# Early reads of the routed results, a regrouped front, and one gate-up moved ahead of the shared expert in a two-layer trunk kernel

## The reference

```python
def trunk_layer(x, cvec, l, lp, ctx, row, col):
    mod = jax.nn.silu(cvec) @ lp['w_mod'] + lp['b_mod']
    sh1, sc1, g1, sh2, sc2, g2 = jnp.split(mod[:, None, :], 6, axis=-1)
    h = rms_norm(x, lp['g_pre1']) * (1.0 + sc1) + sh1
    m, new_cache = token_mixers(h, lp, lam_init, ctx, row, col)
    x = x + g1 * rms_norm(m, lp['g_post1'])
    h = rms_norm(x, lp['g_pre2']) * (1.0 + sc2) + sh2
    x = x + g2 * rms_norm(moe(h, lp), lp['g_post2'])

def moe(h, lp):          # 32 experts, 4 chosen for each token, and one shared expert
    ...
    gu = jnp.einsum('nd,edf->nef', t, lp['w_exp_gu'])
    a = jax.nn.silu(gu[..., :EXPERT_FF]) * gu[..., EXPERT_FF:]
    a = (a * combine[..., None].astype(a.dtype)).reshape(-1, N_EXPERTS * EXPERT_FF)
    routed = a @ lp['w_exp_down'].reshape(N_EXPERTS * EXPERT_FF, D_MODEL)
    sgu = t @ lp['w_sh_gu']
    shared = (jax.nn.silu(sgu[:, :SHARED_FF]) * sgu[:, SHARED_FF:]) @ lp['w_sh_down']
    return (routed + shared).reshape(B, T, D)
```

## Time and profile before

| | |
|---|---|
| three runs | 2102.24, 2106.28, 2112.89 us (median 2106.28) |
| profiled execution | 2108.57 us, its span 2106.4 us |
| PE, PE weight loads, DVE, ACT, POOL busy | 89%, 66%, 61%, 49%, 21% of the span |
| mean granted TensorE clock | 0.948 |
| weights of the experts | 128 gate-up and 64 down transfers of 1 MB |
| reads of `y_rows` | 12 transfers of 1 MB |

### The profile page before, as it was taken

One profiled execution on the slowest core, in us unless ns is written; L12 is line 12 of the kernel. 1 busy time (PEld: TensorE's weight loads), 2 busy tenths in 40 slices (PEclk: granted clock), 3 DMA queues, 4 the chain that ended last, 5 costly groups with the idle time before them and its releaser, 6 DMA issues. The chain is left out here.

```text
span 2106.4 us, 27239 instructions
## 1 busy us (share of the span) xinstructions
PE 1884.7 (89%) x9282; PEld 1393.5 (66%) x9282; DVE 1283.1 (61%) x1827; ACT 1040.4 (49%) x1713; POOL 451.5 (21%) x422
## 2 busy tenths in 40 slices
PE   4999899899998999999649999979999799999991
PEld 2987566788877566666438865668888666666661
DVE  2244567644436688888753455675444467888885
ACT  2333235633335478777533412464333437787782
POOL 0001511310000434444200043114000042343430
PEclk8999999999998999999869999999999989999996
DMA  7534464133334599999834434503333248999984
GB/s 259 175 120 123 154 226 156 47 120 120 121 109 181 178 359 354 345 348 347 295 99 143 136 118 143 200 6 98 123 120 120 106 174 309 355 351 339 350 313 177
DMA packets 145349, 416.91 MB, mean 198 GB/s; under 512 B 26704, under 2 KB 37232, under 8 KB 119152
## 3 DMA queue, kind: packets, MB, share of 16 engines
q1 hardware_dynamic: 125136, 379.76, 51.8%
q0 software_dynamic: 17952, 33.74, 4.8%
q10 hardware_dynamic: 2176, 2.27, 0.4%
HBM read 408.80 MB, written 32.15 MB: 209 GB/s over the span
## 5 line engine op out<-in xcount | busy, mean ns | idle before, releaser
L1648 DVE TENSOR_TENSOR W_split<-W,W_split 128x2048 fp32r<-128x2048 f32 (+2 forms) x92 | 216.2, 2352 | 423.8 <-ACT W_split L1253 423.8
L2190 PE MATMUL psum<-W_split,qT_split 128*128 128x512 f32 (+3 forms) x1536 | 411.4, 380 | 16.2 <-PEq L2519 8.0
L1253 ACT ACTIVATE W_split<-W 128x2048 fp32r<-128x2048 f32 (+2 forms) x92 | 170.0, 1854 | 385.2 <-PE psum L2190 385.2
L2190 PEld LDWEIGHTS psum<-W_split,qT_split 128*128 128x128 f32 x1536 | 284.7, 190 | 71.8 <-issue 16.5
L2190 PE MATMUL psum<-W_split,scratch_split 128*128 128x512 f32 x864 | 280.7, 396 | 0.0
L2190 PE MATMUL psum<-W_split,hT_split 128*128 128x512 f32 x576 | 214.6, 400 | 5.8 <-DVE scratch_split L1843 5.8
L2461 PE MATMUL psum<-W_split,zf_split 128*96 128x512 f32 x512 | 202.8, 396 | 0.0
L2190 PEld LDWEIGHTS psum<-W_split,scratch_split 128*128 128x128 f32 x864 | 162.4, 189 | 38.7
L2190 PE MATMUL psum<-W_split,kT_split 128*128 128x512 f32 (+3 forms) x480 | 177.7, 370 | 0.0
L1173 POOL DMA_INDIRECT zf<-token_rows,vm x56 | 123.6, 2206 | 48.4 <-POOL vm L1170 48.4
L2190 PEld LDWEIGHTS psum<-W_split,hT_split 128*128 128x128 f32 x576 | 109.7, 191 | 31.8 <-DVE scratch_split L1843 6.3
(11 more groups left out here) (353 smaller groups left out, 3872.0 us busy)
## 6 DMA issues: line engine op xcount, KB each, us to landing
W<-in_w_exp_gu SPq DMA_DIRECT2D x128, 1024.0 KB, 11.6
W<-in_w_exp_down SPq DMA_DIRECT2D x64, 1024.0 KB, 11.2
W<-in_w_in SPq DMA_DIRECT2D x60, 1024.0 KB, 5.1
W<-in_w_mod SPq DMA_DIRECT2D x40, 1024.0 KB, 5.3
W<-in_w_br SPq DMA_DIRECT2D x16, 1024.0 KB, 5.1
zf<-y_rows SPq DMA_DIRECT2D x12, 1024.0 KB, 7.1
W<-in_w_out SPq DMA_DIRECT2D x8, 1024.0 KB, 5.1
W<-in_w_mod SPq DMA_DIRECT2D x3, 2048.0 KB, 17.1
```

The lines of the kernel that those rows point to most:

```text
L1253: nc.scalar.activation(high(j), piece(SPLITS[j]), ACT.Copy).then_inc(S["high_ready"], 1)
L1648: V.tensor_tensor(piece(SPLITS[j], Wr), piece(SPLITS[j]), high(j).bitcast(F32), ALU.subtract).then_inc(S["low_ready"], 1)
L2190: ins = nc.tensor.matmul(bank(job, piece_size(key)[1]), act_part[:, k0 + k, t * P:(t + 1) * P], w_part[:, k, :], start=first and (k, i) == ...
```

## The change

Five edits come together.

1. VectorE sorts the four choices of each token by the tile that holds them (`tile_f`, `rank_f`), and scatters place them in `y_rows` in that order. The first two choices of a token can then not lie in the last two tiles. SP reads them (`load_choices(t, 0, ...)`) when the scatters before the last two have landed, into three buffers that the loop no longer needs; VectorE adds them behind its last loop step. The other two are read behind the last scatters, all three transfers at once except that the third waits for two sums.
2. `gained` multiplies the row by the gate row before the root is known; `residual` needs then one operation behind the root. This holds for both residuals of a layer.
3. The front goes by token tile: two banks a tile, half of the columns scaled and shifted by ScalarE, half by VectorE (`modulate_rest`), and the split by tile.
4. TensorE runs the transposes of gathered tile 0 and its gate-up ahead of the shared down products. ScalarE, VectorE, SP and the plan of banks follow that order; SP asks for the down weights of tile 1 last, and VectorE builds the tables behind the last shared bank.
5. The slot arithmetic is rewritten to give the tile by itself, and `shared` and `shared_T` move to other buffers.

The core of the diff (constants, names of semaphores, buffer addresses and the calls at the program's start left out):

```diff
         def modulate_front(act, u, banks):
 
             act.wait_ge(front_gain[u], 1)
+            for t in range(T):
+                act.wait_ge(front_turned[u], 2 * t + 1)
+                v, cols = min(t, 1), slice(t * P, (t + 1) * P)
+                for k in range(KD // 2):
+                    ins = nc.scalar.activation(hTv[:, k, cols], psum[:, banks[2 * t], k * P:(k + 1) * P], ACT.Identity,
                                                scale=modTv[:, 1, k, v:v + 1], bias=modTv[:, 0, k, v:v + 1])
-                ins.then_inc(front_h[u], 1)
+                ins.then_inc(front_mod[u], 1)
+                act.wait_ge(front_mod[u], t + 1)
+                nc.scalar.activation(h_split_z[0][:, 0:KD // 2, cols], hTv[:, 0:KD // 2, cols], ACT.Copy).then_inc(front_h[u], 1)
+
+        def modulate_rest(dve, u, banks, t):
+
+            v, cols, rest = min(t, 1), slice(t * P, (t + 1) * P), slice(KD // 2, KD)
+            dve.wait_ge(front_gain[u], 1)
+            dve.wait_ge(front_turned[u], 2 * t + 2)
+            for k in range(KD // 2, KD):
+                ins = nc.vector.tensor_scalar(hTv[:, k, cols], psum[:, banks[2 * t + 1], (k - KD // 2) * P:(k - KD // 2 + 1) * P],
+                                              modTv[:, 1, k, v:v + 1], modTv[:, 0, k, v:v + 1], ALU.mult, ALU.add)
+            ins.then_inc(front_wide[u], 1)
+            dve.wait_ge(front_wide[u], 2 * t + 1)
+            nc.vector.tensor_copy(h_split_z[0][:, rest, cols], hTv[:, rest, cols]).then_inc(front_wide[u], 1)
+            dve.wait_ge(front_wide[u], 2 * t + 2)
+            dve.wait_ge(front_h[u], t + 1)
+            nc.vector.tensor_tensor(h_split_z[1][:, :, cols], hTv[:, :, cols], h_split_z[0][:, :, cols].bitcast(F32), ALU.subtract).then_inc(front_split[u], 1)
...
-                    sp.wait_ge(*filled(("y", "s", T - 1, 1)))
-                    load_down(1, expert("w_exp_down", 1))
                     sp.sem_inc(S["gu_half"], 2)
                     sp.wait_ge(S["gu_half"], 3)
                     load_half(0, 0, expert("w_exp_gu", 2))
                     sp.wait_ge(*filled(("gu", 0)))
                     load_half(0, 1, expert("w_exp_gu", 2))
+                    sp.wait_ge(*filled(("y", "s", T - 1, 1)))
+                    load_down(1, expert("w_exp_down", 1))
...
+                    def load_choices(t, half, dst):
+
+                        src = a["y_rows"].rearrange("(t p k) n -> t p k n", t=T, k=TOPK)[t, :, 2 * half:2 * half + 2, :]
+                        sp.dma_start(dst, src).then_inc(S[f"y_{('early', 'late')[half]}_landed{t}"], 16)
+
+                    sp.wait_ge(*job_filled(turns - 2, 1, "gu"))
                     if l + 1 < DEPTH:
-                        sp.wait_ge(*job_filled(turns - 2, 1, "gu"))
                         for i in range(2):
                             load_front(sp, l + 1, i)
+                    for e in range(2):
+                        sp.wait_ge(S[f"y_written{e}"], turns * 16 + 16)
+                        sp.sem_inc(S["sp_steps"], 1)
+                    for t in range(T):
+                        load_choices(t, 0, early_y[t])
                     if l + 1 < DEPTH:
                         sp.wait_ge(*job_filled(turns - 1, 0, "gu", LESS["filled"][0]))
                         for i in range(2, RAW):
                             load_front(sp, l + 1, i)
                     for e in range(2):
-                        sp.wait_ge(S[f"y_written{e}"], turns * 16 + 16)
+                        sp.wait_ge(S[f"y_written{e}"], turns * 16 + 32)
                         sp.sem_inc(S["sp_steps"], 1)
+                    for t in range(T):
+                        if t == T - 1:
+                            sp.wait_ge(S["summed"], 2)
+                        load_choices(t, 1, late_y[t])
...
                     silu_shared(2)
-                    turned_shared(0)
-                    empty_shared(0)
                     act.wait_ge(*filled(("xt", 0, 1)))
                     x_high(0)
-                    for t in (1, 2):
+                    act.wait_ge(*filled(("gu", 0)))
+                    nc.scalar.activation(silu[0:CAP, 0, :], psum[0:CAP, BANK_GU, 0:FF], ACT.Silu).then_inc(S["silu_ready"], 1)
+                    turned_shared(0)
+                    for t in range(T):
                         empty_shared(t)
                     act.wait_ge(S["rows_out"], 16 * T)
                     for h in range(2):
                         gu_high(1, h, 32)
                     act.wait_ge(*filled(("xt", 1, 1)))
                     x_high(1)
-                    act.wait_ge(*filled(("gu", 0)))
-                    nc.scalar.activation(silu[0:CAP, 0, :], psum[0:CAP, BANK_GU, 0:FF], ACT.Silu).then_inc(S["silu_ready"], 1)
...
+                    def gained(rows_m, t, dst):
+
+                        link(V.tensor_tensor(dst, rows_m[:, t], gp[:, min(t, 1)], ALU.mult))
+
+                    def residual(rows_g, n, t):
 
                         dve.wait_ge(S["post_root"], n * T + t + 1)
                         r = rs[:, POST + t:POST + t + 1]
                         link(V.reciprocal(r, r))
-                        link(V.scalar_tensor_tensor(rows_m[:, t], rows_m[:, t], r, gp[:, min(t, 1)], ALU.mult, ALU.mult))
-                        V.tensor_tensor(xv[:, t], xv[:, t], rows_m[:, t], ALU.add).then_inc(S["x_ready"], 1)
+                        V.scalar_tensor_tensor(xv[:, t], rows_g, r, xv[:, t], ALU.mult, ALU.add).then_inc(S["x_ready"], 1)
...
+                    link(V.scalar_tensor_tensor(rt[:, R_SEL, 0], row_base, float(NE), iota, ALU.add, ALU.subtract))
                     link(V.tensor_tensor(tmp, q1, rt[:, R_SEL, 0:1].to_broadcast([P, T, NE]), ALU.mult))
-                    link(V.tensor_tensor(slot, slot, tmp, ALU.add))
-                    link(V.scalar_tensor_tensor(slot, q2, float(1 - CAP * NT), slot, ALU.mult, ALU.add))
+                    link(V.tensor_tensor(tmp, tmp, iota[:, None, :].to_broadcast([P, T, NE]), ALU.add))
+                    link(V.tensor_tensor(tmp, tmp, q2, ALU.add))
+                    link(V.tensor_tensor(q1, q1, q2, ALU.add))
+                    link(V.scalar_tensor_tensor(slot, q1, float(-CAP), pos, ALU.mult, ALU.add))
+                    link(V.scalar_tensor_tensor(slot, slot, float(NT), tmp, ALU.mult, ALU.add))
...
-                    of_choices(slot, slot_f)
+                    of_choices(slot, slot_f.rearrange("p (t k) -> p t k", t=T))
+                    of_choices(tmp, tile_f)
...
+                    V.tensor_copy(entry_u[:, :, 1], place_f.rearrange("p t k -> p (t k)"))
                     V.tensor_copy(slot_u, slot_f).then_inc(S["slots_ready"], 1)
...
+                    gu_low(0, 0, 1)
+                    product_shared(2)
+                    gu_low(0, 1, 2)
+                    x_low(0, 1)
+                    dn_low(0, 3)
+                    product(BANK_GU, 0, T + 1)
+                    empty_shared(0)
+                    empty_shared(1)
+                    empty_shared(2)
...
-                    gu_low(0, 0, 1)
-                    product_shared(2)
-                    gu_low(0, 1, 2)
-                    empty_shared(0)
-                    x_low(0, 1)
-                    dn_low(0, 3)
-                    empty_shared(1)
-                    empty_shared(2)
                     gu_low(1, 0, 3)
                     gu_low(1, 1, 4)
                     x_low(1, 3)
-                    product(BANK_GU, 0, T + 1)
                     turns = turns_of(dve)
...
+                    def add_choices(t, half, src):
+
+                        dve.wait_ge(S[f"y_{('early', 'late')[half]}_landed{t}"], 16)
+                        for k in range(2):
+                            i, n = t * TOPK + 2 * half + k, 2 * T * half + 2 * t + k + 1
+                            V.scalar_tensor_tensor(acc[:, t], src[:, k], weight[:, i:i + 1], acc[:, t], ALU.mult, ALU.add).then_inc(S["summed"], 1)
+                            dve.wait_ge(S["summed"], n)
+
                     post_gains(1)
+                    for t in range(T):
+                        add_choices(t, 0, early_y[t])
                     if l + 1 < DEPTH:
                         low_front(dve, l + 1)
+                        next_norm(0)
+                    residual(late_y[T - 1][:, 0], 1, T - 1)
+                    if l + 1 < DEPTH:
+                        for t in range(1, T):
+                            next_norm(t)
+                            modulate_rest(dve, l + 1, NEXT_BANKS, t - 1)
+                        modulate_rest(dve, l + 1, NEXT_BANKS, T - 1)
...
+                    def turn_first_rows(i):
+
+                        pe.wait_ge(S[f"x_landed{i}"], 16)
+                        for h in range(2):
+                            bank_free(("xt", i, h))
+                        turn_gathered(i)
+
+                    turn_first_rows(0)
+                    pe.wait_ge(*emptied(("xt", 0, 0)))
+                    pe.wait_ge(*emptied(("xt", 0, 1)))
+                    bank_free(("gu", 0))
```

(29 more changed lines are left out.)

148 lines of the change are left out of this document (67 added, 81 removed).

## The result

The changed kernel takes 2113.0 us in the median of 20 runs (2107.64 to 2117.85), the kernel before 2106.34 in the median of 20 (2099.06 to 2116.8). The ratio is 1.0029, with a 95% interval from 1.0016 to 1.0041: a loss of some 6 us (+3 to +9), clear of noise but inside the 0.5% that the prediction called no change. The execution profiled after took 2113.40 us, its span is 2111.4.

The account below looks back on a forecast made before the run. The tile loop was taken as bound by its DMA weight stream, so only its start and the tails count. +1.5 - 2.1 + 20.8 - 7.9 - 10.0 = +2.3, forecast 2110 us, 8-in-10 range 2096 to 2122.

Parts of the forecast that it names:

- the entry: Third shared silu to loop start: gate-up 0 ahead of the shared down products delays the loop 10.4 us a layer, +20.8.
- layer 0's tail: Last eviction to next projection: chain 29.5 us against 42.8, 13.3 less; 3.3 lost to a later first late read; gain 10.0.
- The loop as a block: Tile loop: keeps its 317.3 us, within 2 us, and moves with its start, returning nothing of a delay.
- The rival that the loop recovers: First loop tiles: early weights recover the 10.4 us; all 2090, half 2100; chance 0.20 together with tails giving more.
- its fall for a rival: Gate-up 0 at half clock after idle, 2 to 3 us a layer; with crowded scatters 2121; slower cases together 0.24.
- The 0.43 us pitch: Sign of being wrong: gate-up 0's matmuls on TensorE going at 0.43 us instead of 0.23.
- VectorE's tables: Loop's entry: eleven table operations, 4.9 us, run behind the last shared bank; tile 1's weight subtractions wait behind them.
- Layer 1's tail: Behind layer 1's loop: 16.3 us from first late landing instead of 25.7; 1.5 lost to a later landing; gain 7.9.
- over 5: Sign of being wrong: a final scatter behind the loop taking over 5 us to land.
- That the reads bring nothing: Rival, both tails: early reads land only with the final scatter; +7.9 a layer, 2126 us; chance 0.05.
- Gate row ahead of the root: Mixture side, ahead of the projection: first product falls in VectorE's idle time; -1.05 us a layer (0 to -1.3).
- Turns by token tile: Front by token tile: +1.5 us at program start (0 to +3); in layer 0's tail part of the 13.3 less.

Follow-up runs that it names:

- experiment 1: The changed kernel with the order of before at the loop's entry, all else kept: 2089.8 us, ratio 0.9921 to the kernel before.
- experiment 2: The kernel before with only the new order at the loop's entry and the two shared-expert buffers it needs: 2127.44 us, ratio 1.0106.
- experiment 7: The changed kernel with 24 unread identity transposes on TensorE filling the gaps ahead of gate-up 0: 2108.88 us, ratio 1.0006 to the kernel before.
- experiment 3: The changed kernel with VectorE's eleven table operations back ahead of the third shared product: 2111.62 us, ratio 1.0018 to the kernel before.
- experiment 5: The changed kernel with the three early reads issued behind the final scatters, just ahead of the late ones: 2124.57 us, ratio 1.0085.
- experiment 6: The changed kernel with VectorE's split of the next layer's first weights ahead of the six early sums in layer 0's tail: 2113.97 us, ratio 1.0037.
- Experiment 9: The kernel of experiment 8 with the front of before, by column groups, at the program's start and in layer 0's tail: 2084.64 us, ratio 0.9905.
- experiment 8: The kernel of experiment 1 with both engines' splits of tile 1's weights between the emptyings of the shared banks: 2087.01 us, ratio 0.9906.

## Why the prediction was right, and where it was not

**The balance.** 2110 was said, 2113.0 measured. The two large sides were both right: -18.5 without the entry against -17 (-22 to -11, experiment 1), and +20.8 for the entry against +22 (+17 to +27, experiment 2) and +23 (both profiles). Against the kernel before, the sum had +2.3 and +6 was measured. Three terms priced too low account for the 4 us between: the entry by 1.1 a layer, layer 0's tail by 1.3, layer 1's by 0.5. That they add up so evenly is partly luck, since a stretch without an edit moves by up to 4 us from one profile to the next.

**The loop as a block: right.** The loops of the four kernels with the old order last 316.1 us in the mean, of the seven with the new one 316.6, between 312.9 and 321.3 each. A loop that starts 5 to 12 us later is not shorter. The rival that the loop recovers falls: half of the late start would have been 5 us, and the two means lie 0.5 apart. Single loops differ by more than the 2 us that the prediction allowed; layer 1's was 314.6.

**Gate-up first: size right, one link wrong.** Start of the loop at 33.1 to 33.3 us, 32.1 predicted; the gap, the tables behind the last bank and the splits behind them are all there. Two steps failed. The prediction priced the clock in gate-up 0 at nothing and kept its fall for a rival. It falls, and costs 1.5 us a layer (experiment 7), below the 2 to 3 that the rival allowed; that covers the term's error of 1.1. The 0.43 us pitch was one of the prediction's own signs of being wrong. The Trainium skill ("TensorE: Matmul & The Clock Gate", Part 1) says that TensorE's clock falls after an idle stretch and that sustained activity releases it again. The runs agree only in part: behind waits of 1.0 to 1.9 and 2.2 us with 0.85 us of transposes between them the clock fell in eleven of twelve entries, with the gaps filled it stayed at 1.00, but in layer 1 of experiment 2 it stayed at 1.00 behind the same waits too. So the cost is not fixed: 0 to 2.5 us a layer, by experiment 2's two layers. And the prediction named VectorE's tables as what the splits wait for. They do, but ScalarE's copies arrive only 1.3 us earlier, so the tables alone were worth 0.35 us and not 4.9 (experiment 3). The sum did not show this, since both chains have nearly the same end.

**Early reads: right.** Layer 1's tail was to gain 7.9 and gained 7.4; the chain behind the first late landing was to take 16.3 and takes 15.96. The late landing cost 2.0 us (12.1 from the last eviction against 10.1) where 1.5 was chosen. It goes with the end of the early reads: in all eight profiled layer-1 tails that have them ahead, the final scatter landed 0.76 to 0.95 us behind the third early read, whenever it had been issued. That it waits for them is read from this; no run changed their size. Over these tails the cost is 1.6 to 3.1 us and the gain 6.2 to 7.8, so the profile after is on the good side. In four of them the final scatter took 5.95 to 6.58 us; and layer 0's took 7.6 here; over 5 was one of the prediction's signs of being wrong. That the reads bring nothing is refuted by experiment 5: without their head start the kernel takes 2124.57, close to the 2126 that this rival gave.

**Layer 0's tail: 8.7 where 10.0 was said.** The chain from the first late sum was better than predicted, 28.6 against 29.5. What was too small is the loss ahead of it: 5.5 us (15.4 from the last eviction against 9.9) where 3.3 stood. The final scatter was issued at 1048.97, and the late reads that wait for it went out at 1056.68, 7.7 us later, as much as under the full weight stream. Three megabytes of early reads and two pieces of the next weights were on the DMA engines then. The early reads went out 3.3 us ahead of the last eviction instead of the 5.2 in layer 1, and the third landed 9.3 us behind it instead of 5.8. The scatter landed within 0.5 us of that read, here and in the seven other layer-0 tails with early reads ahead. The Trainium skill ("DMA: Bandwidth & Descriptors", "Issuing engines are not separate DMA queues") says that transfers interleave whoever issued them. That the reads hold the scatter up (7.6 and 4.35 us against 3.3 in experiment 5) agrees; the prediction's conclusion that it would not stand behind the whole of them does not, since in none of the sixteen tails did it land more than 0.5 us ahead of the last early read. VectorE's split hangs on the same read, since it stands behind the third pair of early sums, and it held the late sums 0.4 us longer (experiment 6). In the five other profiles that have this tail unchanged the gain is 8.8 to 9.5 us.

**Gate row ahead of the root: right.** From the output projection's last columns to the start of scaling it takes 12.74 instead of 13.93 us in layer 0 and 12.75 instead of 13.93 in layer 1: -1.2 a layer, -1.05 said. The routing's extra operations show no cost beyond a microsecond of scatter (+0.4 and -1.0 from there to the third silu).

**Turns by token tile: wrong in sign.** The sum left 1.8 us of gain to them in layer 0's tail (13.3 less 7.9 for sums and 3.6 for products). Experiment 9 measures a loss of 0.6. The share of VectorE that was moved ahead of the last norm holds that norm up by 3.3 us (21.6 us behind the first late sum in experiment 8, 18.4 in experiment 9), and what follows it is only 2.7 us shorter (6.9 against 9.6). The 1.4 us at the program's start are as predicted.

## What to carry to other kernels

Take a change of several parts apart before judging it: here a gain of some 18 us and a loss of some 20 us hid each other. The kernel with only the gain had the old order at the entry (2090 us), and reshuffling two lists there gave the rest (2087, 2085 with the old front). When work is moved on one in-order engine, walk the lists of the others past the new wait as well, and where two chains hang on the same event, price the second before calling the first the cause. This loop, bound by its transfers, returned nothing of a late start, so what stands ahead of it counted in full.

## What the hardware showed that was not expected

GpSimd copies a tile's row indices just ahead of each scatter. In layer 1's tail of the changed kernel this took 0.23 us ahead of the last scatter but one and 1.28 ahead of the last, which went out 1 us later for it. The two copies in the time line of GpSimd, and the last scatter on the chain of waits of experiment 8, where its copy took 0.18 us:

```profile
2073.78 0.23 POOL L1208 COPY vm<-vm 96x1 uint32 x1 [3.44 <-ACT zf L1576]
2078.28 1.28 POOL L1208 COPY vm<-vm 96x1 uint32 x1 [2.11 <-ACT zf L1576]
```

```profile
2049.97 6.58 DMA y_rows<-zf,vm
```

The sum on VectorE had started at 2078.23 and takes 1.3 us. In experiment 8 the copy began 0.03 us ahead of the first sum (2048.92 and 2048.95) and took 0.18; in experiment 9 0.07 us behind it (2050.31 and 2050.24) and took 1.25. The Trainium skill ("SBUF — State Buffer", "Who interferes with whom") says that a VectorE instruction with two inputs in SBUF contends with a GpSimd instruction that reads SBUF; these sums have two such inputs, and the copy waits out one of them: it ends 0.05 us behind the sum. The loops show the same. Of the 120 copies of this kind in the kernel before, 68 began while VectorE was in an operation with two inputs in SBUF. They took 0.20 to 2.28 us, and 66 of them ended 0.04 us behind that operation, the other two as much behind a next one that followed at once. The remaining 52 took 0.18 to 0.20. No run took the sums away from the copy alone.

The lost microsecond did not reach the end. The scatter that was held up landed 6.7 us behind the last eviction, in experiment 9 6.6; in the four tails whose copy took 0.18 us (experiments 3, 6, 7 and 8) it went out 1.1 us earlier and landed 7.2 to 7.8 us behind it. It landed with the early reads in either case.
